# Experts ordered by count on the chip, with the widest one's steps placed between the steps of the four smallest

## What is computed

```python
def moe_swiglu(h, w_router, w_gu, w_down):
    logits = (h @ w_router).astype(jnp.float32)
    top_vals, top_idx = lax.top_k(logits, TOP_K)
    gates = jax.nn.softmax(top_vals, axis=-1)
    comb = jnp.sum(jax.nn.one_hot(top_idx, N_EXPERTS, dtype=jnp.float32) * gates[..., None],
                   axis=-2).astype(h.dtype)
    y = jnp.zeros_like(h)
    for e in range(N_EXPERTS):
        y = y + comb[..., e:e + 1] * swiglu(h, w_gu[e], w_down[e])
    return y
```

## Time and profile before

| what | value |
|---|---|
| median of 3 runs | 1688.39 us (1687.82 to 1688.59) |
| the profiled execution | 1692.88 us, of it span 1691.1 us |
| PE, PEld, DVE, ACT, POOL busy | 93%, 77%, 73%, 61%, 7% of the span |
| hi (L421), 422 times | 1916 ns each |
| lo (L759), 422 times | 2290 ns each |
| HBM read | 447.63 MB, 265 GB/s over the span |

### The profile page before, as it was taken

The page is one execution under the profiler, slowest core; times in us unless marked ns, Lnnn a source line. Parts: engine busy times, 40 slices in busy tenths (PEclk is TensorE's granted clock), DMA queues, the critical chain, the costliest instruction groups (busy, mean ns, idle before and its releaser), DMA issues.

```text
span 1691.1 us, 22334 instructions
## 1 busy us (share of the span) xinstructions
PE 1580.5 (93%) x7519; PEld 1306.2 (77%) x7520; DVE 1236.1 (73%) x1035; ACT 1038.7 (61%) x924; POOL 125.8 (7%) x83
## 2 busy tenths in 40 slices
PE   8999989999899878899899999999999998988986
PEld 6887878888798767677688888888888776777774
DVE  6745554444489759999998888855555699898995
ACT  4344344434357438888877777744444688888884
POOL 0000000000000004013030030020000120300000
PEclk9999999999999859999999999999999999999997
DMA  9653545555550309999999989956666599999993
GB/s 348 219 194 105 180 145 198 191 182 186 173 173 17 120 27 344 393 385 391 397 377 377 372 309 373 378 177 222 207 203 212 176 387 397 375 393 395 384 394 151
DMA packets 195693, 449.13 MB, mean 266 GB/s; under 512 B 8621, under 2 KB 17357, under 8 KB 195662
## 3 DMA queue, kind: packets, MB, share of 16 engines
q1 hardware_dynamic: 193324, 444.84, 73.4%
q10 hardware_dynamic: 2338, 3.87, 0.6%
HBM read 447.63 MB, written 1.05 MB: 265 GB/s over the span
## 4 chain that ended last, share of the span: by engine, by line
PE 74%; DVE 11%; DMA 7%; issue 5%; ACT 3%; DVEq 0%; POOL 0%; ACTq 0%; POOLq 0%; SPq 0%
PE bank L1271 15%; PE bank L1264 12%; PE bank L1265 11%; DMA raw<-in_moe_w_gu 7%; PE bank L1353 6%; DVE wlo L759 4%; PE bank L1342 4%; PE bank L1262 4%; DVE y L1002 4%; PE bank L1294 2%; PE bank L1301 2%; PE bank L1295 2%; PE bank L1506 2%; PE bank L1344 2%; PE bank L1345 2%
## 5 line engine op out<-in xcount | busy, mean ns | idle before, releaser
L759 DVE TENSOR_TENSOR wlo<-raw,whi 128x2048 fp32r<-128x2048 f32 x422 | 959.8, 2290 | 284.1 <-ACT whi L421 282.4
L421 ACT ACTIVATE whi<-raw 128x2048 fp32r<-128x2048 f32 x422 | 805.5, 1916 | 410.3 <-PE bank L1271 268.8
L1271 PE MATMUL bank<-wlo,xx 128*128 128x512 f32 x1424 | 390.0, 396 | 2.8 <-DVE wlo L759 2.8
L1264 PE MATMUL bank<-whi,xx 128*128 128x512 f32 x848 | 335.9, 396 | 5.7 <-ACT whi L421 2.3
L1265 PE MATMUL bank<-whi,xx 128*128 128x512 f32 x848 | 333.1, 393 | 0.0
L1271 PEld LDWEIGHTS bank<-wlo,xx 128*128 128x128 f32 x1424 | 268.8, 190 | 69.8 <-DVE wlo L759 13.1
L1262 PE MATMUL bank<-whi,xx 128*128 128x512 f32 x576 | 165.2, 409 | 50.2 <-DVE hT L1211 32.6
L1264 PEld LDWEIGHTS bank<-whi,xx 128*128 128x128 f32 x848 | 160.7, 190 | 41.0 <-issue 3.4
L1265 PEld LDWEIGHTS bank<-whi,xx 128*128 128x128 f32 x848 | 160.9, 190 | 32.9
L385 POOL TENSOR_SCALAR onehot<-mats,slot 128x64 fp32r<-128x64 f32 x56 | 114.6, 2069 | 764.6 <-PE bank L1675 764.6
L1262 PEld LDWEIGHTS bank<-whi,xx 128*128 128x128 f32 x576 | 106.3, 193 | 82.9 <-issue 63.1
(11 more groups left out here) (220 smaller groups left out, 1480.5 us busy)
## 6 DMA issues: line engine op xcount, KB each, us to landing
raw<-in_moe_w_gu SPq DMA_DIRECT2D x224, 1024.0 KB, 7.9
raw<-in_moe_w_down SPq DMA_DIRECT2D x112, 1024.0 KB, 8.1
raw<-in_ffn_w_gu SPq DMA_DIRECT2D x28, 1024.0 KB, 5.1
raw<-in_ret_w_in SPq DMA_DIRECT2D x24, 1024.0 KB, 7.6
raw<-in_ffn_w_down SPq DMA_DIRECT2D x14, 1024.0 KB, 4.8
raw<-in_ret_w_out SPq DMA_DIRECT2D x8, 1024.0 KB, 4.9
raw<-in_conv_w_pw SPq DMA_DIRECT2D x16, 512.0 KB, 4.5
raw<-in_conv_w_pw SPq DMA_DIRECT2D x4, 1024.0 KB, 5.0
```

Source lines behind the costliest of these rows:

```text
L421: nc.scalar.activation(whi[base % SPLIT][:, :], raw[base % RAW][:, :], ACT.Copy).then_inc(hi_done, 1)
L759: nc.vector.tensor_tensor(wlo[base % SPLIT][:, :], raw[base % RAW][:, :], whi[base % SPLIT][:, :].bitcast(f32), ALU.subtract).then_inc(lo_ ...
L1264: nc.tensor.matmul(dst[:, :], xh[:, kc, t, :], wh, start=kc == 0, stop=False)
L1271: last = nc.tensor.matmul(dst[:, :], both, wl, start=False, stop=closing and kc == DC - 1)
```

## The change

The route tables give each expert a place. Expert 0 keeps place 0 (its count is raised by 1000 for the ordering); of the others the widest gets place 7 (`SIDE`), and places 1 to 6 are filled by falling count. DVE works out the permutation with some twenty small operations, and SP, PE, ACT and DVE read expert numbers and needs from `plan`. Places 0, 1 and 2 run as before, one after the other. Then a loop of four rounds (`MAINS`) takes places 3 to 6. A round holds the 7 steps of a main expert and two steps of the side expert (one in the last round), each of the latter between two main steps: products of the side step, down rows of the main step, side turn, gates and ups of the next main step, down rows of the side step, main turn. At the second of a round the main step that follows already belongs to the next expert, so gather, scatter and accumulate lie there.

The side expert's gathered rows have tiles of their own (`xb0`, `xb1`) and so have its one-hot matrices. Its down sums stay apart: the first tile's in banks 6 and 7 over all seven steps, the second's in banks 1 and 3, which its products need too, so DVE adds them to `acc` in SBUF after each side step (`side_sum`, awaited by PE through `tile1_free`). The main experts' scatter uses banks 4, 5, 1 and 3. The main experts' first gate blocks take 8 matmuls where the need is 0. Few-turns now go to banks 0 and 2 instead of 1 and 3. The diff, cut to its core (DVE's and PE's parts; ACT's follow the same order of steps):

```diff
+SOLO, MAINS, SIDE = 3, 4, 7
+B_MAIN = B_MOE + SOLO * MOE_BLOCKS
+S_MAIN = STEPS + SOLO * STEPS
+ROUND = STEPS + 2
...
+        SCAT_MAIN = [bank[4], bank[5], bank[1], bank[3]]
+        SIDE_DOWN = [[bank[6], bank[7]], [bank[1], bank[3]]]
+        SCAT_SIDE = [bank[6], bank[7], bank[1], bank[3]]
...
+            solo(0, 0)
+            sp.wait_ge(order_done, 1)
+            with sp.Fori(1, SOLO) as e:
+                solo(expert_at(e), e)
...
+            def main_round(i, wg, wd):
+                six = ROUND * i
+                with sp.Fori(0, 2) as j:
+                    gu(wg, B_MAIN + 4, j + 1, six + j)
+                    down(wd, B_MAIN + 8, j, six + j)
+                gu(side_g, B_MAIN + 16, 2 * i, six)
+                down(wd, B_MAIN + 20, 2, six)
+                gu(wg, B_MAIN + 22, 3, six)
+                down(side_d, B_MAIN + 26, 2 * i, six)
+                with sp.Fori(0, 3) as j:
+                    gu(wg, B_MAIN + 28, j + 4, six + j)
+                    down(wd, B_MAIN + 32, j + 3, six + j)
...
+            def step_of(base, s, kind_before, kind, six):
+                end_of(s, kind_before, base + 2, six)
+                for b in range(3, 6):
+                    lo(base + b, six)
+                begin(base, s, kind, six)
+                lo(base + 7, six)
+            def side_sum(used, first):
+                dve.wait_ge(pe_done, used)
+                for n in range(2):
+                    cols = slice(n * BANK, (n + 1) * BANK)
+                    if first:
+                        last = nc.vector.tensor_copy(acc[:, cols], SIDE_DOWN[1][n][:, :])
+                    else:
+                        last = nc.vector.tensor_tensor(acc[:, cols], SIDE_DOWN[1][n][:, :], acc[:, cols], ALU.add)
+                last.then_inc(tile1_free, 1)
...
+            def side_y_lo():
+                for n in range(2):
+                    dve.wait_ge(yh_done, 2 * SIDE + n + 1)
+                    cols = slice(n * BANK, (n + 1) * BANK)
+                    nc.vector.tensor_tensor(yl[:, 0, cols], SIDE_DOWN[0][n][:, :], yh[:, 0, cols].bitcast(f32),
+                                            ALU.subtract).then_inc(yl_done, 1)
+                dve.wait_ge(side_yh_done, 1)
+                nc.vector.tensor_tensor(yl[:, 1, :], acc[:, :], yh[:, 1, :].bitcast(f32), ALU.subtract).then_inc(side_yl_done, 1)
+            def main_round(i, kind):
+                six, s = ROUND * i, S_MAIN + ROUND * i
+                with dve.Fori(0, 2) as j:
+                    step_of(B_MAIN + 4, s + 1 + j, kind, kind, six + j)
+                step_of(B_MAIN + 16, s + 3, kind, WIDE, six)
+                step_of(B_MAIN + 22, s + 4, WIDE, kind, six)
+                with dve.If(i < 1):
+                    side_sum(B_MAIN + 28 + 6 * six, True)
+                with dve.Else():
+                    side_sum(B_MAIN + 28 + 6 * six, False)
+                with dve.If(i > MAINS - 2):
+                    side_y_lo()
+                with dve.Fori(0, 3) as j:
+                    step_of(B_MAIN + 28, s + 5 + j, kind, kind, six + j)
+                with dve.If(i < MAINS - 1):
+                    end_of(s + 8, kind, B_MAIN + 48, six)
+                with dve.Else():
+                    end_of(s + 8, kind, None, six)
+                    accumulate(SIDE, SCAT_SIDE, NE)
...
+                with dve.If(i < MAINS - 1):
+                    for b in range(49, 52):
+                        lo(B_MAIN + b, six)
+                    hidden(s + 8, B_MAIN + 50 + 6 * six, 2)
+                    xl_gathered(i + SOLO + 1)
+                    lo(B_MAIN + 52, six)
+                    lo(B_MAIN + 53, six)
+                    y_lo(i + SOLO + 1)
+                    hTl_evac(s + 9, 2)
+                    lo(B_MAIN + 54, six)
+                    lo(B_MAIN + 55, six)
+                    accumulate(i + SOLO + 1, SCAT_MAIN)
+                    lo(B_MAIN + 56, six)
+                    lo(B_MAIN + 57, six)
+                    with dve.If(need_of(dve, i + SOLO + 1) < 1):
+                        begin(B_MAIN + 52, s + 9, FEW, six)
+                    with dve.Else():
+                        begin(B_MAIN + 52, s + 9, FULL, six)
+                    lo(B_MAIN + 59, six)
+                    side_sum(B_MAIN + 58 + 6 * six, False)
...
+            def side_products(base, s, need, six, free):
+                pe.wait_ge(silu_done, 2 * s)
+                pe.wait_ge(tile1_free, free)
+                for half in range(2):
+                    pe.wait_ge(hi_done, base + half + 1 + 6 * six)
+                    block_columns(base + half, bank[1], half, 3, FULL, six)
+                    block_columns(base + half, bank[0], half, 2, FULL, six).then_inc(pe_done, 1)
+                pe.wait_ge(hTl_done, s)
+                for half in range(2):
+                    pe.wait_ge(hi_done, base + 2 + half + 1 + 6 * six)
+                    with pe.If(need > 2):
+                        block_columns(base + 2 + half, bank[3], half, 3, FULL, six)
+                    with pe.Else():
+                        block_columns(base + 2 + half, bank[3], half, 3, HALF_FULL, six)
+                    block_columns(base + 2 + half, bank[2], half, 2, FULL, six).then_inc(pe_done, 1)
...
+            need = need_of(pe, SOLO)
+            pe.wait_ge(xel_done, SOLO + 1)
+            main_gates(B_MAIN, need, 0)
+            scatter_before(SOLO)
+            pe.wait_ge(hTl_done, S_MAIN)
+            main_ups(B_MAIN, S_MAIN, need, 0)
+            pe.wait_ge(res_done, 2 * SOLO + 8)
+            onehot_turn(1, bank[5]).then_inc(ohT_ps, 1)
+            pe.wait_ge(side_onehot_done, 1)
+            onehot_turn(2, bank[4], side_onehot).then_inc(side_ohT_ps, 1)
+            gather(0, SIDE_DOWN[0], side_onehot)
+            gather(1, SIDE_DOWN[1], side_onehot).then_inc(side_gather_ps, 1)
+            main_turn(S_MAIN, need)
+            pe.wait_ge(ohT_done, SOLO + 1)
+            pe.wait_ge(side_ohT_done, 1)
+            clear(DOWN[0])
...
+            with pe.Fori(0, MAINS) as i:
+                six, s = ROUND * i, S_MAIN + ROUND * i
+                need = need_of(pe, i + SOLO)
+                with pe.Fori(0, 2) as j:
+                    main_step(B_MAIN + 4, s + 1 + j, need, six + j)
+                side_products(B_MAIN + 16, s + 3, side_need, six, 2 * i + 1)
+                main_rows(B_MAIN + 20, 0, False, need, six)
+                main_rows(B_MAIN + 21, 2, False, need, six)
+                side_turn(s + 3, side_need)
+                pe.wait_ge(silu_done, 2 * (s + 4))
+                main_gates(B_MAIN + 22, need, six)
+                pe.wait_ge(hTl_done, s + 4)
+                main_ups(B_MAIN + 22, s + 4, need, six)
+                with pe.If(i < 1):
+                    pe.wait_ge(side_xl_done, 1)
+                    clear(SIDE_DOWN[0])
+                side_rows(B_MAIN + 26, side_need, six)
+                with pe.If(i > MAINS - 2):
+                    nothing(bank[6])
+                    nothing(bank[7]).then_inc(side_done, 1)
+                main_turn(s + 4, need)
+                with pe.Fori(0, 3) as j:
+                    main_step(B_MAIN + 28, s + 5 + j, need, six + j)
+                with pe.If(i < MAINS - 1):
+                    side_products(B_MAIN + 46, s + 8, side_need, six, 2 * i + 2)
+                    pe.wait_ge(silu_done, 2 * (s + 9))
+                    pe.wait_ge(onehot_done, i + SOLO + 2)
+                    gather(0).then_inc(gather_ps, 1)
+                    main_rows(B_MAIN + 50, 0, False, need, six)
+                    main_rows(B_MAIN + 51, 2, True, need, six)
+                    side_turn(s + 8, side_need)
+                    pe.wait_ge(xel_done, i + SOLO + 2)
+                    next_need = need_of(pe, i + SOLO + 1)
+                    main_gates(B_MAIN + 52, next_need, six)
+                    pe.wait_ge(hTl_done, s + 9)
+                    scatter(i + SOLO + 1, 1, SCAT_MAIN)
+                    main_ups(B_MAIN + 52, s + 9, next_need, six)
+                    pe.wait_ge(res_done, 2 * (i + SOLO + 1) + 8)
+                    onehot_turn(1, bank[4]).then_inc(ohT_ps, 1)
+                    side_rows(B_MAIN + 56, side_need, six)
+                    main_turn(s + 9, next_need)
+                    pe.wait_ge(ohT_done, i + SOLO + 2)
+                    clear(DOWN[0])
+                with pe.Else():
+                    pe.wait_ge(side_yl_done, 1)
+                    scatter(SIDE, 2, SCAT_SIDE, side_onehotT)
+                    pe.wait_ge(hTl_done, s + 8)
+                    main_rows(B_MAIN + 46, 0, False, need, six)
+                    main_rows(B_MAIN + 47, 2, True, need, six)
+            pe.wait_ge(res_done, 2 * SIDE + 8)
+            scatter(NE, 1)
...
+    first = np.where(e == 0, 1000, 0)
+    rank_at = np.array([0, 2, 3, 4, 5, 6, 7, 1])
+    route = np.concatenate([(e[None, :] < e[:, None]).reshape(-1), first, rank_at]).astype(f)
```

435 lines of the change are left out of this document (362 added, 73 removed).

## The result

| | before | after |
|---|---|---|
| median | 1689.12 us (8 runs, 1687.82 to 1691.47) | 1700.28 us (8 runs, 1695.45 to 1704.01) |
| the profiled execution | 1692.88 us, span 1691.1 | 1704.01 us, span 1702.2 |
| mean granted clock | 0.975 | 0.969 |

The ratio is 1.0064, with an interval of 1.0046 to 1.0081: 0.6% slower, beyond the 0.2% that a measurement of this kernel can tell. The forecast was 1695.4 us, 0.4% slower, with a range of 1675 to 1709. The profiled execution is the longest of the eight, and that of before lies above all of its eight; the spans differ by 11.1 us, the medians by 11.2. The eight runs of after lie in two groups, four at 1695.5 to 1697.8 us with a mean clock of 0.973 to 0.977 and four at 1702.8 to 1704.0 with 0.969 to 0.972, and the profile is of the second, so the median run may well have fewer falls of the clock than what follows shows.

A forecast was written before the change was run, and what follows sets the result against it. A few step was taken as a PE-DVE ring of 14.85 us, DMA costing little. New stretches summed to 697.1 against 704.4 (-7.3); ordering +1, clock +12 and control flow +1 made +7: 1695.4 us, range 1675 to 1709.

The forecast's parts named there:

- Term 1: From the gather of place 3 to its first turn: 25 us, plus 2.6 for DVE evacuating four banks.
- Term 5: Seven side_sum on DVE behind hidT_product, fully exposed on the ring: 1.4 us each, 9.8 in all.
- Term 6: Splitting the side's sums between ACT and DVE in the last round: 3.6 us on DVE.
- Term 7: From the last turn to the end: 23.5 us before, 1.3 less because the side scatter fits PE's wait.
- Term 8: Ordering the experts on the chip with small DVE operations around the first expert's start: +1 us.
- Term 9: PE's clock falling after longer waits behind each side_sum and the entry: eight times 1.5 us, +12.
- Term 10: Added Ifs and reads of plan on DVE and ACT over four rounds: +1 us, upper bound 15.
- Rival B: Each change of expert or round costs DVE or ACT a fetch or table load: +13, 1708 us; chance 0.19.
- A: PE's clock stays up behind the longer waits, so its +12 goes: 1683.4 us; chance 0.22.
- C: Light steps' lo done under side products, so PE's work alone counts: 1606 us; chance 0.14, weak form included.
- weak form: Only the side sums hide, -10 us, and the clock falls go with them: 1675 us; within C's 0.14.
- D: The experts' order differs, such as a main expert on the full path; time about the same; chance 0.02.

The follow-up runs named there:

- e4: The kernel before with only half of each expert weight block loaded: 1677.93 us, ratio 0.9936 to the kernel before.
- e10: e8 with only half of each expert weight block loaded: 1652.39 us, ratio 0.9774 to the kernel before.
- e1: The changed kernel with side_sum moved in front of hidT_product on DVE: 1694.06 us, ratio 1.003 to the kernel before.
- e5: The changed kernel with PE's loop over the four rounds written out: 1695.35 us, ratio 1.0026 to the kernel before.
- e8: The changed kernel with the edits of e1, e2, e5 and e6 together: 1653.92 us, ratio 0.9777 to the kernel before.
- e7: The changed kernel's ordering on the chip with the old loop over eight experts, no interleaving: 1690.38 us, ratio 1.0006 to the kernel before.
- e2: The changed kernel with the arms for full experts left out of PE's main blocks: 1699.38 us, ratio 1.0072 to the kernel before.
- e3: The changed kernel with six useless matmuls of zeros on PE ahead of its wait for hidT_lo: 1703.86 us, ratio 1.0082 to the kernel before.
- e6: The changed kernel with hidT_hi and hidT_lo ahead of the next hi and lo in main steps: 1686.37 us, ratio 0.9979 to the kernel before.

## Why the prediction was right, and where not

The sign and the size came out (0.64% for 0.41%), and its structure too, but one term was off by a factor of about ten, and others made up for part of it. Span against span, forecast +7.0, measured +11.1. Counted between markers:

- *What bounds the kernel before*: right. A ring of 14.85, DMA 1.1 above it; e4 puts DMA's whole cost at 11.8 us, and e10 shows it gone once the steps are mixed. All the distances that were forecast for the mixing stand: a light step 14.77 (14.85), a pair 44.55 to 45.02 (44.7), a pair with a change of expert 52.04, 53.59 and 52.04 (52.7; the middle one has a fall of the clock in it). Over twenty light steps the 0.08 is 1.6 less.
- *Term 1, the entry*: 30.95, where the forecast's sum leaves 29.4 for it on this count (708.3 - 7.3, less 649.9 for the other terms and 21.7 for the end), 1.5 more; the step behind it 16.89 where 2.6 for four banks and 1.5 for the clock had made 18.95 of it. PE's wait there was 3.58, with 4.2 forecast. Net 0.5 less.
- *Term 5, side_sum*: the mechanism was right and shows in the trace to the queue position; 1.2 each, not 1.4. e1 shows it by removal. At the loop's start it is covered by PE's own lateness.
- *Term 6, the split*: 4.0, with 3.6 forecast. With the sum and a fall of the clock, the last pair and the step behind it are 66.7 together, 0.7 over the forecast's 66.05.
- *Term 7, the end*: 21.6 from the last marker, 23.0 before: -1.4, forecast -1.3. The match is luck, for the wait of 1.78 ahead of the side scatter lies in it, and in e5 and e8, which don't have it, the end is 19.6 and 19.3.
- *Term 8, ordering*: +1 forecast; the first expert ends 1.5 earlier (733.47 against 734.95), and e7 as a whole is the same as before.
- *Term 9, the clock*: right that waits near 3 lead to falls, mostly (two of the three alike ones of 2.74 to 2.83). The price was mis-sized: 2.8 in a step, not 1.5. It had been read from a fall behind 1429.00, where the clock was at 0.73 over 3 us, half-way back; here it stayed at 0.50 through the ups. Falls behind the first pairs cost 5.5 instead of 4.5.
- *Term 10, control flow*: this step failed. It was +1, with 15 as the upper bound; the loop's starts alone took 6.68, 5.41 and 6.72 more than a light step, 18.8, where sum, clock and term 10 had 9.7 for them; e5 puts the loop's share at 10.9, and the end is 2.0 shorter there. The prediction read the start of today's loop on ACT and reasoned about Ifs on ACT and DVE. It didn't look at PE, the engine with by far the most instructions. At PE's own loop start of before it would have found no gap at all (1447.04, above), so no row of that kernel had the price; the error is that a row of the old loop was carried over to a new one, whose stop falls on PE and within the ring. Rival B had the rule and the place right (it costs where it falls behind `hidT_product`) but named the wrong engines and took up to 2 us a place where 4.1 to 6.0 stand in the trace. e5 shows that the loop's form is the cause. The Trainium skill (Runtime: NRT & Kernel Launch, Instruction fetch mechanics) says that a taken branch to code outside what the engine holds makes it wait for a fetch. The waits that e5 removes and the instruction packets, 20 before and 63 after, agree with it; that the target wasn't held is not shown by itself. It was set aside in the forecast because one row of another engine spoke against a large price.

Together: over the forecast by 9.1 at the loop starts, 1.5 at the entry, 0.7 at the split and 0.5 behind the first pairs; under it by 2.5 for the ordering, 2.1 in the step behind the entry, 1.6 in the pace of the light steps and 1.7 in the rest (three light steps of 14.55, the last of 14.25, the pairs): 3.9 over, and the spans show 4.1. That the forecast lay within 5 us is partly luck: 11.8 us of errors on one side met 7.9 on the other, which have nothing to do with them.

Of the rivals, A (the clock stays up) is refuted by the 0.50 rows of the profiled execution; it is what e1 restores at two places. C (mixing works better) was refuted in its form of 1606 us: even e8 has 14.02 a light step, not 12.5. (The 1606 is itself some 5 too high: it takes the 82 off the time of before, though it was reckoned against the forecast's sum.) Its weak form, the side sums hidden and the falls with them, is e1, 1694, and not 1675, since the loop's starts stay. D (another order) is refuted by the trace: the four main experts take few steps, beside a wide one. The Trainium skill (Perfetto Trace Analysis, Optimization Strategy) advises that interleaving regimes with different most-contended engines may improve performance. Here it does so only once the ring is free of what was put on it: 0.6% slower as made, 2.2% faster in e8.

## What to carry to other kernels

When steps of two kinds are interleaved, the shorter kind is a ring over two engines, and anything placed between its links counts in full wherever no other engine is late anyway, and can count again through the clock; look for a wait of the same engine one place earlier (here 5.99 us on DVE) and put the work there. Before lengthening a loop body on the engine that bounds the kernel, compare the instruction queues' packets on the page before and after, which say whether code is fetched again, look for idle time without a releaser where the loop starts over, and write the rounds out if they are few. Fixes on one path don't add up when they lie over each other, so try them together before judging the idea.

## What was new about the hardware

- Where PE's loop over the four rounds started over, PE stood idle for 4.13 to 6.04 us in three places of after (5.2 to 6.1 in e1, e2, e3 and e6), with 16.4 KB an instruction packet (1.03 MB in 63). A body shortened so far that 10 fewer packets are fetched costs the same, and the body written out four times costs nothing of the kind. In the kernel before PE's loop over the experts starts over without idle time (1447.04), with 20 packets in all.
- The clock falls to the 1.2 GHz level (0.50 of 2.4) after waits that don't tell it apart: 2.74 twice, once with a fall and once without. At one place of the step with the change of expert it fell in round 1 of after behind waits of 0.39 and 0.52 (the step of 25.48), and not in rounds 0 and 2 behind 0.41 and 0.53, and 0.41 and 0.55 (the two of 23.93). In e5 it falls there in all three rounds, first behind waits of 0.47 and 0.73, and once behind one of 1.63, though waits of 1.53 to 1.62 never had it in the kernel before. The Trainium skill (TensorE: Matmul & The Clock Gate, A second HAM failure mode) describes a bf16 kernel in which short idle times between groups of matmuls were enough to make the clock swing between its levels. These rows have falls behind waits well under 1 us too; that those waits are their cause is not shown. What exactly decides between two like waits stays open.
- A fall costs 2.8 us of a step when it comes ahead of 16 matmuls that nothing else hides, as much as the whole wait of 2.74 to 2.83 ahead of it.
